# Loading the input by quarters of its features and reordering the small steps at a two-block kernel's head

## The reference

```python
sh1, sc1, g1, sh2, sc2, g2 = adaln_params(c[:, None, :], w_mod[i], b_mod[i])   # silu(c) @ w_mod + b_mod, in six
csh1, csc1, cg1, csh2, csc2, cg2 = adaln_params(c_ctx, w_mod[i], b_mod[i])
hx = modulate(x, sh1, sc1)              # x * (1 + sc1) + sh1
hc = modulate(h_ctx, csh1, csc1)        # the context, 256 x 1024
...
k_c, v_c = project_kv(hc, w_qkv)
q_l = apply_rope(project_q(hx, w_qkv), cos, sin)
k_l, v_l = project_kv(hx, w_qkv)
k_l = apply_rope(k_l, cos, sin)
k_all = jnp.concatenate([k_c, k_l], axis=1)
v_all = jnp.concatenate([v_c, v_l], axis=1)
y_lat = diff_head_out(latent_diff_attention(q_l, k_all, v_all, lam), attn_subln_g[a], lam_init, attn_w_o[a])
```

## Time and profile before

| | us |
|---|---|
| median of 3 runs | 1248.38 (1246.42 to 1248.42) |
| the profiled execution | 1250.41 |
| its span in the trace | 1248.7 |
| TensorE busy | 1158.2 (93%) |
| VectorE busy | 772.7 (62%) |
| ScalarE busy | 570.5 (46%) |

### The profile page before, as it was taken

How to read it: one execution, slowest core, us unless ns; L and a number is a source line. 1 busy time by engine, 2 the same in 40 slices (tenths; PEclk the granted TensorE clock), 3 DMA queues, 4 the chain that set the end, 5 groups by cost and what they waited for, 6 DMA issues and landing times.

```text
span 1248.7 us, 15377 instructions
## 1 busy us (share of the span) xinstructions
PE 1158.2 (93%) x6348; PEld 971.8 (78%) x6348; DVE 772.7 (62%) x868; ACT 570.5 (46%) x783; POOL 62.1 (5%) x118
## 2 busy tenths in 40 slices
PE   4899979899999977699999899999999899999998
PEld 2677756679998756599998687787787788997886
DVE  1586668578878739687554465435656567665444
ACT  2542327565444213354443446654665356545342
POOL 2011120000111100000000000000000000000000
PEclk8999989999999878799999989999999999999999
DMA  9956680157998844387555657878652265655550
GB/s 310 382 193 221 227 292 21 68 183 236 321 339 288 273 165 149 120 266 250 178 184 180 153 122 162 155 151 163 135 200 75 71 219 184 186 183 186 185 177 34
DMA packets 119431, 236.80 MB, mean 190 GB/s; under 512 B 5569, under 2 KB 60162, under 8 KB 119234
## 3 DMA queue, kind: packets, MB, share of 16 engines
q1 hardware_dynamic: 105458, 186.26, 49.8%
q0 software_dynamic: 13904, 49.56, 11.7%
HBM read 234.75 MB, written 1.05 MB: 189 GB/s over the span
## 4 chain that ended last, share of the span: by engine, by line
PE 82%; DVE 6%; DMA 4%; ACT 3%; issue 2%; SPq 2%; DVEq 0%; ACTq 0%
PE ps L1676 17%; PE ps L1677 16%; PE ps L1678 16%; PE ps L1715 7%; PE ps L1714 7%; PE ps L1713 7%; PE ps L1795 2%; DVE modraw L1079 2%; DMA modraw<-in_w_mod 1%; PE ps L1931 1%; PE ps L1944 1%; DMA raw<-in_w_in 1%; DMA mod<-in_w_mod 1%; ACT wH L558 1%; DVE wL L1000 1%
## 5 line engine op out<-in xcount | busy, mean ns | idle before, releaser
L1000 DVE TENSOR_TENSOR wL<-raw,wH 128x1024 fp32r<-128x1024 f32 x328 | 397.6, 1222 | 309.9 <-ACT wH L558 308.5
L558 ACT ACTIVATE wH<-raw 128x1024 fp32r<-128x1024 f32 x328 | 343.1, 1057 | 440.7 <-PE ps L1678 295.9
L1676 PE MATMUL ps<-wH,aH 128*128 128x512 f32 (+1 forms) x624 | 252.6, 405 | 17.8 <-DVE aL L1028 9.9
L1677 PE MATMUL ps<-wL,aH 128*128 128x512 f32 (+1 forms) x624 | 245.8, 394 | 0.0
L1678 PE MATMUL ps<-wH,aL 128*128 128x512 f32 (+1 forms) x624 | 245.3, 393 | 0.0
L1713 PE MATMUL ps<-aH,wH 128*128 128x256 f32 x768 | 219.0, 285 | 0.0
L1715 PE MATMUL ps<-aH,wL 128*128 128x256 f32 x768 | 217.3, 283 | 0.0
L1714 PE MATMUL ps<-aL,wH 128*128 128x256 f32 x768 | 217.3, 283 | 0.0
L1676 PEld LDWEIGHTS ps<-wH,aH 128*128 128x128 f32 x624 | 120.3, 193 | 52.6 <-issue 24.8
L1713 PEld LDWEIGHTS ps<-aH,wH 128*128 128x128 f32 x768 | 147.4, 192 | 0.7 <-issue 0.5
L1714 PEld LDWEIGHTS ps<-aL,wH 128*128 128x128 f32 x768 | 147.4, 192 | 0.7 <-issue 0.7
(11 more groups left out here) (295 smaller groups left out, 1227.2 us busy)
## 6 DMA issues: line engine op xcount, KB each, us to landing
raw<-in_ffn_w_in SPq DMA_DIRECT2D x88, 512.0 KB
modraw<-in_w_mod POOLq DMA_DIRECT2D x80, 512.0 KB, 6.1
raw<-in_w_in SPq DMA_DIRECT2D x32, 1024.0 KB
raw<-in_ffn_w_out SPq DMA_DIRECT2D x22, 1024.0 KB
raw<-in_w_up SPq DMA_DIRECT2D x16, 1024.0 KB
raw<-in_w_down SPq DMA_DIRECT2D x16, 1024.0 KB
mod<-in_w_mod SPq DMA_DIRECT2D x8, 1024.0 KB, 12.5
raw<-in_attn_w_qkv SPq DMA_DIRECT2D x8, 1024.0 KB
```

Source lines behind the costliest of these rows:

```text
L558: nc.scalar.activation(wH[:, n % WS, :], raw[:, (n // 2) % RAW, (n % 2) * 1024:(n % 2) * 1024 + 1024], ACT.Copy).then_inc(w_hi, 1)
L1000: V.tensor_tensor(wL[:, n % WL, :], raw[:, (n // 2) % RAW, (n % 2) * 1024:(n % 2) * 1024 + 1024], wH[:, n % WS, :].bitcast(fp32), ALU.subt ...
L1676: T.matmul(outp, xh, h, start=first, stop=False)
L1677: T.matmul(outp, xh, l, start=False, stop=False)
```

## The change

- x is loaded in four pieces of 256 features (`x_in` is now four semaphores), each behind its block of w_mod, instead of whole behind the first.
- POOL's twelve loads of small rows and its load of 16 columns of w_in, which stood first in its queue, now stand behind the vector loads 0 to 3.
- Beside the modulation, VectorE runs `mod_put(c)` ahead of `adv(2c)`, and both VectorE and ScalarE run `adv(2c + 1)` behind the split of x instead of ahead of it.
- VectorE takes `low_ctx(0)` ahead of the first rotation and `low_ctx(1)` ahead of the second; `adv(10)` comes ahead of both rotations.
- `rotate` raises `acc_out` after the four products that read PSUM, and a new semaphore `rot_done` after the sums; `heads` waits for that one where the unit is rotated.
- The turns: q1's stands behind sub-step (2, 2) instead of behind chunk 2; those of the K units behind sub-steps 1 and 2 of chunks 3 and 4, one unit each, instead of two behind chunks 3 and 4.

```diff
@@ SP @@
                 for w in range(2):
                     sp.dma_start(mod0[...], by_k(a["w_mod"][0])[...]).then_inc(mod0_in[m], 16)
-                if m == 0:
-                    sp.dma_start(x[:, :, :], a["x"].rearrange("b (t p) d -> p (b t) d", p=P)).then_inc(x_in, 16)
+                cols = slice(256 * m, 256 * m + 256)
+                sp.dma_start(x[:, :, cols], a["x"].rearrange("b (t p) d -> p (b t) d", p=P)[:, :, cols]).then_inc(x_in[m], 16)
@@ POOL: rows2 (12 loads) and lrw now follow vec_load(1) to vec_load(3) and precede ln_load(0) @@
-            pool.wait_ge(rows_T, 1)
...
             pool.wait_ge(mod_acc, NMOD0)
             pool.wait_ge(w_hi, 11)
             vec_load(0)
...
             for v in range(1, IN_QKV):
                 vec_load(v)
+            for j, nm in enumerate(("norm_mix_2", "norm_mlp_2", "norm_ple_2")):
+                pool.dma_start(rows2[8 * j:8 * j + 8, :], ...).then_inc(rows2_in, 16)
...
             ln_load(0)
@@ ScalarE @@
                 mod_copy(c)
-                for j in range(2):
-                    adv(2 * c + j)
+                adv(2 * c)
                 act.wait_ge(mod_out, c + 1)
                 hi(GROUPS["x"] + c, aH[:, 2 * c:2 * c + 2, :], mod=mc(c))
+                adv(2 * c + 1)
...
                     if (c, j) == (2, 1):
                         heads_out(0)
+                    elif (c, j) == (2, 2):
+                        heads_out(1)
+                    elif c in (3, 4) and j >= 1:
+                        heads_out(c - 1, (2 * j - 2, 2 * j - 1))
...
                         nc.scalar.activation(v[...], pair(un + j), ACT.Copy).then_inc(acc_out, 1)
-                        if c == 4:
-                            heads_out(c - 1, (2 * j, 2 * j + 1))
                 adv(n + 4 * c + WS + 3)
-                if c <= 3:
-                    heads_out(c - 1)
@@ VectorE @@
             for c in range(NMOD0):
+                mod_put(c)
                 adv(2 * c)
-                mod_put(c)
-                adv(2 * c + 1)
                 lo(GROUPS["x"] + c, ...)
                 hcount[0] += 1
+                adv(2 * c + 1)
...
                 else:
+                    at_least(dve, rot_done, {0: 0, 1: 1, 3: 2, 5: 3}[un])
                     for t in range(TT):
...
-                    link(ins)
+                    ins.then_inc(acc_out, 1)
+                    dve.wait_ge(acc_out, un + 1)
                     for t in range(TT):
...
-                    ins.then_inc(acc_out, 1)
+                    ins.then_inc(rot_done, 1)
...
-            adv(8)
-            adv(9)
+            for j in range(8, 11):
+                adv(j)
+            low_ctx(0)
             rotate(UNITS["q"], n + 7, False)
-            adv(10)
-            low_ctx(0)
+            low_ctx(1)
+            adv(11)
             rotate(UNITS["q"] + 1, n + 8, False)
-            adv(11)
-            for j in range(1, 4):
+            for j in range(2, 4):
                 low_ctx(j)
@@ TensorE @@
             def x_group(j):
+                pe.wait_ge(x_in[j], 16)
...
             def heads(unit):
-                pe.wait_ge(acc_out, UNITS["q"] + unit + 1)
+                if unit in (2, 4):
+                    pe.wait_ge(acc_out, UNITS["q"] + unit + 1)
+                else:
+                    pe.wait_ge(rot_done, {0: 1, 1: 2, 3: 3, 5: 4}[unit])
...
                     elif (c, sub) == (2, 1):
                         pe.wait_ge(t_lo, GROUPS["ctx"] + 4)
                         heads(0)
+                    elif (c, sub) == (2, 2):
+                        heads(1)
+                    elif c in (3, 4) and sub in (1, 2):
+                        heads(2 * c - 5 + sub)
...
-                if c == 2:
-                    heads(1)
-                elif c < 5:
-                    heads(2 * c - 4)
-                    heads(2 * c - 3)
```

More of the change, by code:

```diff
@@ L303, in build @@
         t_done, t_f, t_hi, t_lo = sem("t_done"), sem("t_f"), sem("t_hi"), sem("t_lo")
-        x_in, ctx_in, rows_in, cst_in, cst2_in = (sem(n) for n in ("x_in", "ctx_in", "rows_in", "cst_in", "cst2_in"))
-        small_in = sem("small_in")
+        x_in = [sem(f"x_in{i}") for i in range(NMOD0)]
+        ctx_in, rows_in, cst_in, cst2_in = (sem(n) for n in ("ctx_in", "rows_in", "cst_in", "cst2_in"))
+        small_in, rot_done = sem("small_in"), sem("rot_done")
         mod0_in = [sem(f"mod0_in{i}") for i in range(NMOD0)]
@@ L499, in _ @@
                 vec_load(v)
+            for j, nm in enumerate(("norm_mix_2", "norm_mlp_2", "norm_ple_2")):
+                pool.dma_start(rows2[8 * j:8 * j + 8, :], a[nm].rearrange("l (r p) -> (l r) p", p=P))\
+                    .then_inc(rows2_in, 16)
+            pool.dma_start(rows2[24:32, :], a["gla_out_norm_2"].rearrange("l h (r p) -> (l h r) p", p=P)).then_inc(rows2_in, 16)
+            pool.dma_start(rows2[32:33, :], a["moba_k_norm_2"]).then_inc(rows2_in, 16)
+            pool.dma_start(rows2[33:34, :], a["moba_q_norm_2"]).then_inc(rows2_in, 16)
+            for j in range(6):
+                w = (a["ln_g"], a["ln_b"])[j % 2]
+                k = (0, 2, 3)[j // 2]
+                pool.dma_start(rows2[34 + 8 * j:42 + 8 * j, :],
+                               w[k // 2, k % 2:k % 2 + 1, :].rearrange("l (r p) -> (l r) p", p=P)).then_inc(rows2_in, 16)
+            with nc.allow_non_contiguous_dma(reason="16 columns of w_in"):
+                pool.dma_start(lrw[:, :, :], a["w_in_2"][0].rearrange("(k p) n -> p k n", p=P)[:, :, LR0:LR0 + GRANK])\
+                    .then_inc(lrw_in, 16)
             ln_load(0)
@@ L1876, in _ @@
             mod_select(0)
-            pe.wait_ge(x_in, 16)
             x_group(0)
```

14 lines of the change are left out of this document (removed).

## The result

| | us |
|---|---|
| changed kernel, median of 8 | 1238.08 (1235.89 to 1242.64) |
| kernel before, median of 8 beside it | 1247.22 |
| ratio, 95% interval | 0.9937 (0.9916 to 0.9959) |
| the profiled execution | 1241.02, span 1239.3 |
| TensorE's clock over the span | 0.968 (before 0.964) |

The change is worth 7.9 us by the ratio, 9.1 between the medians and 9.4 between the two profiled executions. Medians, ratios and means leave out the few executions that ran far slower than the rest, such as 1460.95 and 6361.5 us of run r14.

What follows compares the result with a forecast made beforehand. With TensorE busy 93% of the span, only its waits and slow-clock stretches could be won. Terms 2.5 + 0.4 - 1.25 + 0.3 + 1.95 - 0.65 - 0.8 + 1.95 = 4.4 us took 1248.38 to 1244.0, range 1241.7 to 1247.2.

Steps and rivals of the forecast that it cites:

- Step 1: Head, modulation: x in quarters and small loads moved bring w_mod's third block and its product 2.5 us earlier, to 32.3.
- that of the small loads: Head: POOL's small row loads and w_in columns take 5.4% of 16 engines over 25 us, 1.35 us.
- their 1.2: Head: two quarters instead of all of x stand ahead of w_mod's third block, 1.2 us less.
- the queue's own: Rival, head: the DMA hole at 16 to 19 us stays, 1.3 us less gain, 1245.3; within a shared chance of 0.18.
- upper bound of 4.1: Head: gain of 4.1 us if the slow clock after the third block's wait went too.
- Step 2: First K chunk: context ahead of rotations, bank released early; K product 2.9 us earlier, new X-half wait 1.2, gain 1.65.
- Step 3: Chunks 2 to 5: turns of Q and K moved inside the chunks; gain grows from 1.65 to 4.4 us.
- a sign of being wrong: Whole kernel: the forecast is wrong if more loads of w_mod are waited for.
- More than the forecast: Before attention: a first load in time, or a slow stretch gone, 1.6 to 2.1 us more; chance 0.13.
- The slower rival: Head: each quarter of x holds the queue longer than its bytes do; at 2 us each, 1251.0; chance 0.05.
- clock falls would eat the gain: Step 2's new wait or chunk boundaries: one fall costs 1.6 us, 1245.6; two leave 1.2, 1247.2, chance 0.14.

Runs made afterwards that it cites:

- r14: Changed kernel with the turns of Q and K back behind the chunks: 1239.41 us, ratio 0.9964.
- r12: Kernel before with only POOL's small loads moved behind the vector loads, x loaded whole: 1239.24 us, ratio 0.9955.
- r6: Changed kernel with x loaded whole again, small loads still moved: 1238.67 us, ratio 0.9957.
- r2: Kernel before once more, no edit, as a control: 1246.96 us, ratio 1.0017.
- r4: Kernel before with only the turns moved inside the chunks: 1245.34 us, ratio 0.9992.
- r5: Kernel before with four extra unread TensorE products in each of two waits of the head: 1246.99 us, ratio 1.0007.
- r3: Kernel before with x in quarters and the small loads moved, nothing else: 1241.27 us, ratio 0.9958.
- r7: Changed kernel with POOL's small loads back at the head of its queue: 1241.68 us, ratio 0.9974.
- r10: Changed kernel with two extra VectorE operations, about 2.5 us, ahead of attention's first maximum: 1244.90 us, ratio 0.9996.
- r15: r14's kernel with four extra unread TensorE products in attention's sub-step 13: 1236.93 us, ratio 0.9921.
- r8: Changed kernel with chunk 5's last vector step moved behind attention's first maxima: 1237.04 us, ratio 0.9934.
- r9: Changed kernel with one extra VectorE operation, about 1.2 us, ahead of attention's first maximum: 1241.49 us, ratio 0.9971.
- r1: Changed kernel once more, no edit: 1237.24 us, ratio 0.9940.
- r11: r8's kernel with q1 rotated straight behind q0: 1237.85 us, ratio 0.9936.
- r16: Changed kernel with turns behind the chunks, extra products in attention, last vector step late and q1 rotated first: 1233.86 us, ratio 0.9894.

## Why the prediction was wrong

The waits of the head were summed nearly right, partly by luck: its terms are off in both directions. The failed step is how that sum was carried to the end.

**Step 1, "The block lands 2.5 us earlier, at 32.3."** It landed at 30.8, 4.0 earlier and before it was wanted, and TensorE's own work, forecast to be done at 30.5, set 31.9. The term that was mis-sized is that of the small loads, priced at 1.35 by their share of the engines' time: they held the block up by 3.5 in the mean (r12 and r6 against before, r2, r4 and r5). The quarters won 0.7 to 1.1 of their 1.2, but with the small loads gone nobody waits for the block, and r3 against r12 and r6 measure them at nothing. A share of time says what a queue took, not how the other queue ran beside it: the rival of a hole that is "the queue's own" fell in r7. Taken out by themselves (r12) the small loads give 5.6 us, with an interval of 2.9 to 8.5; put back (r7) they cost (0.9974 - 0.9937) x 1247 = 4.6, with intervals that overlap. I also kept the slow clock behind this wait and set its going as the upper bound of 4.1. It went. The Trainium skill (TensorE: Matmul & The Clock Gate, "HAM oscillation — how this bites in real kernels") describes a DMA wait followed by a throttled start; the first profile of before agrees, with 0.60 behind 2.2 us of wait. But shorter waits at the same place, 1.23 us in r2 and 1.36 in r7, were followed by full clock.

**Step 2, gain 1.65 after it.** K product forecast at 60.05, measured at 58.84; X half 65.7 and 64.34, its wait 1.2 and 2.47. The wait grew since I let the C half end at 64.5, 4.45 after its start, which is its length before, in a stretch at 0.51; 12 products of 0.24 take 2.9. I took no fall of the clock in the wait. In the changed kernel's two profiles and in r6, r10 and r15 there is none. In r8, r9 and r14, with the same head, a stretch of 3.4 us at half clock begins even ahead of this wait, 0.4 to 1.3 us after the K product's start. This is r8's:

```profile
59.70:63.10 3.40, 3.07 (x8) 1.88 (x6) 3.40 (x6) 0.00 (x0) 0.00 (x0) 0.50 1.04 396
```

It costs nothing, as I had it for faster C products: the X half starts 5.5 after the K product in r8, r9 and r14 as in the changed kernel.

**Step 3, the chunks.** X halves in chunks 3 and 4 wait for no rotation and the C half of chunk 4 stands right behind the vector sum, as forecast. VectorE waits for w_mod until 120.12 (forecast 120.9), the vector sums come at 133.19 and 153.99 (forecast 133.95 and 154.75), all 0.8 early. The chain of loads paces this stage as I had it. But four loads of w_mod are waited for in the chain where there were two, which I had named as a sign of being wrong. And the turns push chunk 3's vector sum back by 2.8 and all loads behind it, which I priced at 1.6 and set against a boundary that r14 shows to be as short without them; so they are no part of the gain. r14's expectation credits turns and ScalarE's shorter chain with 2.8 of the 4.4; at the first maximum they cost 2.15, while context order and early release, for which step 2 had a loss of 0.85, gave 3.71. That the total of 4.14 lies so near 4.4 is luck.

**"After attention's start the diff changes no instruction but POOL's moved loads, so what the head gains is carried along or lost there."** This is the step that failed. On the way there, TensorE ends chunk 5 at 167.2, 6.6 earlier, but attention gains only 4.14, since the last vector step waits for its load; I had the 4.4 there by the vector sum alone and never looked at the loads behind it. Then time is won in attention, for the same instructions: it takes 63.0 us in both profiles of the changed kernel, 65.6 and 68.7 in those of before, 2.6 to 5.7 that the sum put at nothing. What changed is the clock: 6.2 us of attention at half clock instead of 10.2 and 20.5. Over all 18 profiles the length follows that time, a delay of 1.2 us ahead of attention brings both back (r9: 65.6 and 11.5), and products that only fill a wait take a stretch and 1.5 us away (r15). The last 2.6 us of the 9.4, behind the layer norm, are another matter. Both profiles have the same half-clock time there, 62.8 and 63.1 us, and the kernel before alone differs from itself by more, 1002.2 and 998.0 us from the layer norm to the end. They may be nothing but that spread.

How much of the whole is clock can be estimated over executions. The mean time of before over 32 executions is 1245.87 at a mean clock of 0.9678, so 2 x 0.0322 x 1245.87 = 80 us at half clock; the changed kernel has 1238.84 and 76.5 us, its repetition 1238.33 and 74.3. If TensorE sets the time throughout, a microsecond at half clock does half a microsecond's work. Of the 7.0 and 7.5 us between the means, (80.2 - 76.5) / 2 = 1.9 and (80.2 - 74.3) / 2 = 2.9 are then clock, and 5.2 and 4.6 are left for waits. Taken against r2's twelve executions instead (1247.12 at 0.9663, 84.1 us at half clock), the repetition gains 8.8, of which 4.9 are clock and 3.9 waits. So the waits are worth 3.9 to 5.2, about the forecast's 4.4, and the rest is clock. This is bookkeeping over the whole span, argued and not shown instruction by instruction, and r5 shows that half-clock time in the head is not worth its half.

**The rivals.** "More than the forecast" came true in its direction. It had 0.13, and its size was one slow stretch gone, 1.6 to 2.1 us; its lower end of 1241.7 is even 0.2 below what 4.4 + 2.1 gives. Two stretches of the head and the one at 161 went together, but r5 shows that the head's are worth nothing by themselves; what made the size was attention, which no rival named. The slower rival, quarters that don't overlap, is refuted: counted from the first block, the third lands 1.1 earlier with quarters (r3) than without (r12), not later. That clock falls would eat the gain is refuted at the boundaries between chunks, where the changed kernel kept 1.00 from its first rise to 172.7, and to 173.1 in r1. It is half true in attention, where it eats what r14 gains and a part of what r11 gains.

**Still open.** Why the half-clock stretches behind the first layer norm fall differently from one execution to the next: from there to the end every kernel here takes between 994.0 and 1002.2 us, with 48.5 to 72.6 of them at half clock, whatever its head did. Why r5's third block came late. Why r8's and r11's early start doesn't show in their ratios, though 4.0 and 3.7 us of it are there at the layer norm in their profiles. Whether the small loads in their new place hold up the last vector load. Whether the turns' place does harm in the time, or r14's attention only falls badly for the clock: r14 and the changed kernel overlap.

## What to carry to other kernels

Look for small loads on another queue in the stretch where the big loads set the time: they may hold the other queue up for longer than their share of the engines says (3.5 us in the mean for a share of 1.35 here), and moving them is a cheap edit (0.9955 by itself). After summing the waits, read where TensorE's clock is at half speed before, in the stages behind the change too: a shift of their start moves these stretches about, and where TensorE sets the time that is won or lost with no instruction changed. Take more than one profile of a kernel before you build on where its clock halves. And when a sum comes out right, measure its parts: here four parts were off by up to 5 us and cancelled.

## What was not expected of the hardware

- The length of attention follows its half-clock time over 18 profiles: 63.0 to 63.5 us for 3.4 to 6.8 (64.1 with extra products), 65.1 to 66.0 for 10.2 to 12.5, 68.7 to 68.8 for 20.5.
- In the changed kernel's head TensorE waits for no load, and then the distance from the clock's first rise (at 25.9 in the changed kernel's profile) to the first K product hardly varies: 32.96 there, and 33.02, 33.12, 32.82, 33.16, 32.81 and 32.75 in r1, r6, r8, r10, r14 and r16, with 33.3, 33.3 and 33.7 in r11, r15 and r9. In both profiles of before, r4 and r5 it is 37.6, 33.5, 35.6 and 35.2. Such a head starts attention at nearly the same place against the clock's changes, which goes with the 63.0, 63.0 and 63.1 of the changed kernel, r1 and r6, and with the longer attention behind a delay of 1.2 us. That the one causes the other is argued, not shown.
- A wait of 2.47 us of TensorE for an X half (58.8 to 64.4) left the clock at 1.00, and one of 2.2 us in the kernel before was followed by 0.51. Ahead of the first K product a wait of 1.8 us (2.15 in r9) was followed by half clock in r8, r9 and r14 and by full clock in the changed kernel, r1 and r6. The length of the wait by itself doesn't decide it.
- 30 packets of the software queue, 0.07 MB, took 27.3% of 16 engines' time in 3 us, and the total fell from 348 to 257 GB/s.
